# Causal attention on TensorE: the value products of two units issued together, and VectorE's store of a unit one place later

## The reference

```python
def dilated_attention_branch(qkv, gate, q_norm_w, k_norm_w, rel_bias):
    ...
    for window, dilation in DILATED_PATTERNS:
        o_p, lse_p = dilated_pattern(q, k, v, rel_bias, window, dilation)
    ...
    wts = jax.nn.softmax(jnp.stack(lses), axis=0)
    o = jnp.sum(wts[..., None] * jnp.stack(outs), axis=0)
    ...
    return o * jax.nn.silu(gate.astype(jnp.float32))
```

## Time and profile before

| | us |
|---|---|
| median of 3 runs (1573.58 to 1575.53) | 1574.15 |
| the profiled execution | 1572.48 |
| its span, first to last instruction | 1570.70 |
| the stage's value products, first to last start | 1336.4 to 1470.6 |

### The profile page before, as it was taken

One profiled execution on the slowest core, in us unless ns is written; L12 is line 12 of the kernel. 1 busy time (PEld: TensorE's weight loads), 2 busy tenths in 40 slices (PEclk: granted clock), 3 DMA queues, 4 the chain that ended last, 5 costly groups with the idle time before them and its releaser, 6 DMA issues.

```text
span 1570.7 us, 30384 instructions
## 1 busy us (share of the span) xinstructions
PE 1499.0 (95%) x12386; PEld 1301.2 (83%) x12386; DVE 818.6 (52%) x1511; ACT 627.6 (40%) x1297; POOL 411.3 (26%) x509
## 2 busy tenths in 40 slices
PE   6999999969999899998999999999997998999998
PEld 6999789958788667776799999888896887888887
DVE  5239510068888667644430715362515776887531
ACT  5322011147777467633332212332334543766300
POOL 0212221110000076623202212221207674333430
PEclk9999999989999999999999999999999999999999
DMA  8313112200000033166402335432120120221332
GB/s 245 53 55 108 54 32 73 75 12 1 1 1 0 2 108 72 53 144 184 135 14 38 55 83 91 62 58 50 28 78 26 30 71 23 84 68 57 110 121 81
DMA packets 84465, 103.50 MB, mean 66 GB/s; under 512 B 25375, under 2 KB 68543, under 8 KB 84328
## 3 DMA queue, kind: packets, MB, share of 16 engines
q1 hardware_dynamic: 84328, 101.56, 25.2%
HBM read 78.40 MB, written 23.12 MB: 65 GB/s over the span
## 4 chain that ended last, share of the span: by engine, by line
PE 50%; DMA 3%; DVE 2%; ACT 2%; POOL 1%; issue 1%; SPq 1%; ACTq 0%; DVEq 0%; POOLq 0%
PE s_ps L362 21%; PE s_ps L1174 8%; PE s_ps L2624 2%; PE s_ps L2610 2%; PE s_ps L2599 2%; PE s_ps L2002 1%; PE s_ps L1987 1%; DMA qT<-s_gate 1%; DMA vT<-s_out_b 1%; PE s_ps L2038 1%; PE s_ps L992 1%; PE s_ps L2051 1%; PE s_ps L973 1%; PE s_ps L2600 1%; PE s_ps L2587 1%
## 5 line engine op out<-in xcount | busy, mean ns | idle before, releaser
L328 POOL TENSOR_TENSOR p_w_lo<-p_w_raw,p_w_hi 128x2048 fp32r<-128x2048 f32 (+1 forms) x27 | 125.1, 4635 | 545.8 <-ACT p_w_hi L312 545.8
L362 PE MATMUL s_ps<-p_w_hi,w_out_hi 128*128 128x256 f32 (+1 forms) x640 | 182.0, 284 | 0.7 <-ACT p_spill L387 0.6
L362 PE MATMUL s_ps<-p_w_hi,w_out_lo 128*128 128x256 f32 (+1 forms) x640 | 179.7, 281 | 0.0
L362 PE MATMUL s_ps<-p_w_lo,w_out_hi 128*128 128x256 f32 (+1 forms) x640 | 179.6, 281 | 0.0
L362 PE MATMUL p_ps<-p_w_hi,hT_hi 128*128 128x256 f32 x576 | 163.5, 284 | 3.0 <-DVE p_w_lo L322 3.0
L362 PE MATMUL p_ps<-p_w_hi,hT_lo 128*128 128x256 f32 x576 | 162.6, 282 | 0.0
L362 PE MATMUL p_ps<-p_w_lo,hT_hi 128*128 128x256 f32 x576 | 162.6, 282 | 0.0
L362 PEld LDWEIGHTS s_ps<-p_w_hi,w_out_hi 128*128 128x128 f32 x640 | 120.6, 188 | 1.7 <-ACT p_spill L387 1.1
L362 PEld LDWEIGHTS s_ps<-p_w_lo,w_out_hi 128*128 128x128 f32 x640 | 120.8, 189 | 0.0
L362 PEld LDWEIGHTS s_ps<-p_w_hi,w_out_lo 128*128 128x128 f32 x640 | 120.6, 188 | 0.0
L312 ACT CAST p_w_hi<-p_w_raw 128x2048 fp32r<-128x2048 f32 (+1 forms) x28 | 53.4, 1908 | 164.2 <-DMA p_w_raw<-w_in 85.7
(11 more groups left out here) (299 smaller groups left out, 3655.0 us busy)
## 6 DMA issues: line engine op xcount, KB each, us to landing
p_w_raw<-w_in SPq DMA_DIRECT2D x27, 1024.0 KB, 8.4
s_gate<-p_spill SPq DMA_DIRECT2D x48, 128.0 KB, 1.8
kbT<-x SPq DMA_DIRECT2D x8, 512.0 KB, 7.1
b_w_raw<-w_out SPq DMA_DIRECT2D x8, 512.0 KB, 4.9
qT<-s_gate SPq DMA_DIRECT2D x8, 512.0 KB, 6.6
qT<-x SPq DMA_DIRECT2D x8, 512.0 KB, 3.6
s_x<-qT SPq DMA_DIRECT2D x8, 512.0 KB, 4.8
c_table<-s_line SPq DMA_DIRECT2D x8, 512.0 KB, 3.6
```

Of the source, the lines that this page charges most:

```text
L328: ops.tensor_tensor(self.w_lo[:, c % 2, :, 0:w], self.raw[:, :, 0:w], self.w_hi[:, c % 2, :, 0:w].bitcast(F32), ALU.subtract).then_inc(sel ...
L362: last = self.nc.tensor.matmul(out, lhs, rhs, start=(kt == 0 and i == 0), stop=(kt == KT - 1 and i == 2))
```

## The change

PE no longer calls `values(u - 1)` behind the turns of each unit. Behind the turns of every second unit (u = 2, 4, ...) it calls `values(u - 2)` and `values(u - 1)`, one right after the other; after the loop stand the two that are left, with the turn of the output's first tile between them as before. DVE stores unit u-3 where it stored u-2, and three units after the loop where it stored two. No instruction is added or dropped.

```diff
             turn_probs(u)
             for h, part in preps(u):
                 turn_prep(h, part)
-            if u >= 1:
+            if u >= 2 and u % 2 == 0:
+                values(u - 2)
                 values(u - 1)
+        values(n_units - 2)
         pe.wait_ge(max_ready, n_units)
         out.turn(pe, 0)
         values(n_units - 1)
...
-            if u >= 2:
-                store(u - 2)
+            if u >= 3:
+                store(u - 3)
             if u + 2 < n_units:
                 bias_and_max(u + 2)
             empty(u)
             for h, part in preps(u):
                 low(h, part)
-        store(n_units - 2)
-        store(n_units - 1)
+        for u in range(n_units - 3, n_units):
+            store(u)
         yield
```

## The result

The changed kernel takes **1564.5 us** (median of 19 runs, 1559.15 to 1572.75); the kernel before, beside it on the same chip, 1573.83 (19 runs, 1572.0 to 1580.76). The ratio is 0.9937, its 95% interval 0.9926 to 0.9948: some 9.9 us, or 0.63%, faster (the two medians lie 9.3 apart; the interval allows 8.2 to 11.6). Forecast were 1564.2 us and a gain of 10.0.

What follows compares the result with a forecast made beforehand. PE was taken to set the pace. The terms 10.6 + 3.4 - 2.9 - 0.95 - 0.2 = 9.95, say 10.0 us, off the median of 1574.15 gave 1564.2 us, with a range of 1561.0 to 1568.5.

Steps and rivals of the forecast that it cites:

- The price of a change of tile: PE going to the small tile for `values` and back: 0.34 us a call, 31 calls fewer, 10.6 us saved.
- Quarters 0 and 1: Next head's preparation, at units 0 and 1: moved values cover PE's 0.57 us stall, six times, 3.4 us saved.
- Quarters 2 and 3: Next head's preparation, at units 3 and 4: a new PE stall of 0.42 us in 7 heads, 2.9 us lost.
- Rival D: No new stall between quarters 2 and 3, as ACT and DVE answer quicker: 12.9 us gained, 1561.3 us; chance 0.05.
- The root: First head, next head's preparation: PE waits 1.13 us for ACT's chain instead of 0.17, 0.95 us lost once.
- The tail: Last units: PE waits 0.44 us for ACT's copy of unit 61, less wait before unit 63's turns; net 0.2 lost.
- Edit 2: DVE stores one place later: taken as 0 us, between 0 and one store (about 0.4) at the end.
- Rival C: Slower: PE stands within each pair for the store of the unit three back; 14.0 us lost, 1578.2; chance 0.05.
- The sum and the head: All terms together: 9.95, say 10.0 us saved; a head of eight units falls from 17.55 to about 16.0 us.

## Why the prediction was right

It was right in its sign, its size (10.0 against 9.9 us) and in what makes it. That the sizes agree to 0.1 is luck: with the terms as measured below, the sum is 10.6 + 2.2 − 2.9 − 1.0 − 0.2 = 8.7, and the interval of 8.2 to 11.6 can't tell 8.7 from 10.0. Step by step, from the traces:

**The price of a change of tile, 0.34, and 31 of them.** Confirmed. On the timeline above, the stretch of a pair from the end of the last transpose's load (1373.74 + 0.79 = 1374.53) to the second load of the next scores (1376.01) is 1.48 us; the prediction's 0.08 + 0.34 + 36 × 0.029 gives 1.46. The forecast of 33 calls is met, and the idle ahead of the loads, forecast as 5.5, is 5.4. Parting the pairs gives the price back, and the full tile removes it. The Trainium skill's sentence that a change of tiling mode drains the engine ("TensorEngine Tiling (Array Packing)", Key Properties), which the prediction weighed against the pulled-ahead loads, agrees with both experiments, and with the gaps behind scores, which grow from 0.07 to 0.37 with the product ahead.

**Quarters 0 and 1, 3.4 us. This is the term that was mis-sized.** The stall was to vanish, 0.57 covered by 0.59. In the six heads it is 0.48, 0.26, 0, 0.24, 0 and 0.24: 1.22 in place of 6 × 0.57 = 3.42, so 2.2 were saved and not 3.4. The prediction took the chain's length from the kernel before and let PE alone change. But DVE, which holds the remainder, also moved. Before, its maximum of 896 columns began 0.56 ahead of quarter 0's load (1385.87 against 1386.43):

```profile
1385.87 1.09 DVE L2677 CUSTOM_DVE_ANT_0 c_prob<-s_ps,c_table 128x896 f32<-128x896 f32 x1 [0.61 <-PE s_ps L2600]
```

After, it is 0.39 ahead in the heads without a stall (1386.02 against 1386.41) and 0.10 to 0.12 ahead in three of those with one (1370.10 against 1370.20); in the first of the six, with 0.48, it comes 0.13 behind that load. The copy of the unit before and its store stand close ahead of it, and PE arrives at the quarter sooner. The remainder ends at 1371.83 + 0.69 = 1372.52, and quarter 1's load follows 0.12 later. A cover of 0.59 over 0.57 has 0.02 to spare; it should have been given as a bound, not as a full saving.

**Quarters 2 and 3, a new stall of 0.42 in 7 heads.** Exact: 0.42 in each of the seven (0.419 to 0.425), shown on the timeline as 0.39 at 1378.64 (the pitch of a load is taken off differently). Rival D falls.

**The root, a wait of 1.13 in the first head.** Two waits, 0.44 and 0.74 on the timeline:

```profile
1342.84 0.47 PEld L2587 LDWEIGHTS s_ps<-ident,c_twice 128*128 128x128 f32 x4
...
1348.06 0.19 PEld L2599 LDWEIGHTS s_ps<-c_kk,c_q_hi 128*128 128x128 f32 x1 [0.44 <-DVE c_q_lo L2666]
1349.56 0.53 PEld L2610 LDWEIGHTS s_ps<-ident,c_prob 128*128 128x128 f32 x5 [0.74 <-ACT c_prob L2741]
```

They sum to 1.18, and unit 6's turns start 1349.56 − 1342.84 = 6.72 after quarter 2, where 6.73 was given as ACT's chain. One of the two waits stands at another place than was said.

**The tail.** From unit 63's scores to the first load of the output product it took 7.93 us before and 7.76 after: 0.17 gained, with one change of tile (0.34) in it, so 0.17 lost beside it (forecast 0.2).

**Edit 2 at nothing.** Right in the changed kernel, where DVE's wait for the values is 1.8 us in 3 times and PE waits for no store. The store alone shows what carries that zero: with pairs, PE reaches the unit's products later than the store that they need. Rival C's price was real for the later store without pairs.

**The sum and the head.** By the terms as measured, a head should fall by 4 × 0.34 + 0.57 − 1.22/6 − 0.42 = 1.31; it fell from 17.55 to 16.16 on the mean, 1.39. The stage fell by 8.24 in the two profiles. About 1.15 of what is missing to the 9.9 is a half-clock stretch in the profiled execution of the changed kernel at the stage's start, in code that is the same in both. From the first scores' load to quarter 1 it takes 6.96 before and 8.10 after; in the run with more work on DVE, which had no such stretch, 6.96, and its stage was 133.88, 9.84 less than before. With the 1.15 the stage of the changed kernel fell by 9.4, which is 0.7 more than the measured terms add up to (8.7); where the 0.7 comes from was not traced.

## What to carry to other kernels

Where a tile smaller than the array makes products cheap, count the changes to it and back as work of the bounding engine, measured as a round trip (0.34 us here, of which the profile labels only 0.17 as idle); then do more between two changes. Each such move also moves the waits: list for every engine behind the bound one what it stands in front of, since here the store's place decided between 9.9 us gained and 31.8 lost. And a cover that fits with 0.02 us to spare is an even chance, not a saving.

## What the runs showed of the hardware that was not expected

**The granted clock moves one program's time more than the doubt about the change does.** In five of the 19 runs of the changed kernel, mean clocks of 0.980, 0.982, 0.985, 0.987 and 0.990 stand beside 1572.75, 1566.08, 1564.5, 1561.38 and 1559.15 us: 0.9% from end to end. In the profiled execution of the changed kernel the clock stands at 1.2 GHz in places where the kernel before has less of it. Two windows, columns as in the earlier trace rows, of the changed kernel:

```profile
1177.50:1206.00 28.50, 20.87 (x272) 18.07 (x274) 11.28 (x25) 8.78 (x28) 19.68 (x24) 0.52 0.06 18
1334.50:1339.00 4.50, 3.47 (x17) 2.94 (x15) 2.88 (x8) 2.65 (x7) 0.62 (x1) 0.62 0.79 247
```

and the same two places in the kernel before:

```profile
1177.50:1206.00 28.50, 17.76 (x309) 14.91 (x309) 13.45 (x30) 14.13 (x45) 19.77 (x25) 0.88 0.11 32
1332.50:1337.00 4.50, 3.13 (x40) 2.68 (x41) 3.19 (x8) 3.44 (x11) 1.09 (x2) 1.00 0.81 248
```

The first stretch lies ahead of the stage, in code the change doesn't touch: 0.52 against 0.88. The second is the stage's start: 0.62 against 1.00. In the run with more work on DVE the half-clock stretch ahead of the stage was 17.1 us long, in the changed kernel's second profile 13.7, in its first 27.3, and in the kernel before 6.8. So single profiles are to be compared by stage, and ratios by many runs.

**DVE began an instruction 0.18 to 0.20 late without a releaser that explains it.** In every second head of the changed kernel, the maximum that reads 896 columns starts late: at 1370.10, although the store ahead of it ended at 1369.62 + 0.28 = 1369.90. It needs scores whose last product ended at 1369.26 + 0.34 = 1369.60 and the turns of the unit three back, which were done earlier; the releaser given, PE's turns of the moment, is neither. Yet in the three late heads it starts within 0.03 of ACT's copy of that turn (1370.07). In the next head it follows the store directly (1386.02), 0.26 ahead of that copy, and with one more short instruction ahead of it, in all of them: the last four heads from quarter 0 to quarter 0 are 15.99 each. The stall at quarter 1 comes with it, but for the first of the six heads, where the maximum follows the store directly and is late all the same. What delays it is open; nothing was tried for it alone.
